# Where the split activations begin in SBUF: new start places for H, L, HH, HL and for the small matmul operands, in a float32r transformer kernel

## The reference

```
# first block (depth 1)
h = rms_norm(x);  proj = h @ w_in + b_in            # 1024 -> 4864
x += (gated sum of an RWKV-7 branch and an RG-LRU branch) @ w_mix_out
x += cross_attention(rms_norm(x), rms_norm(mem))    # w_cq, w_ckv, w_co
x += (gelu(conv(h @ w_in[:2816])) * h @ w_in[2816:]) @ w_ffn_out
# second block (depth 2), for each layer
x += 0.5 * norm(swiglu(norm(x), w13, w2))           # stage a: 1024 -> 2 x 2816 -> 1024
x += norm(token_mixing(norm(x)))                    # stage m: three attentions, gates, w_out
x += norm(cross_attention_2(norm(x), norm(mem)))    # stage c
x += 0.5 * norm(swiglu(norm(x), w13, w2))           # stage b
```

## Time and profile before

| | |
|---|---|
| time, median of 3 runs (lowest to highest) | 2054.82 us (2053.24 to 2056.61) |
| the profiled execution | 2060.7 us |
| its span, first to last instruction | 2058.5 us |
| PE busy | 2021.5 us (98%) |
| DVE busy | 1353.8 us (66%) |
| ACT busy | 1090.1 us (53%) |
| share of PE in the chain that ended last | 90% |
| granted TensorE clock over the span | 0.999 |

### The profile page before, as it was taken

One profiled execution on the slowest core, in us unless ns is written; L12 is line 12 of the kernel. 1 busy time (PEld: TensorE's weight loads), 2 busy tenths in 40 slices (PEclk: granted clock), 3 DMA queues, 4 the chain that ended last, 5 costly groups with the idle time before them and its releaser, 6 DMA issues.

```text
span 2058.5 us, 34241 instructions
## 1 busy us (share of the span) xinstructions
PE 2021.5 (98%) x13588; PEld 1798.6 (87%) x13588; DVE 1353.8 (66%) x1909; ACT 1090.1 (53%) x1739; POOL 50.0 (2%) x47
## 2 busy tenths in 40 slices
PE   7999999999999999999999999999999999999998
PEld 7989988999888889899988888888899999887887
DVE  6776866777566667866766554655477677756554
ACT  5846555554454454555456444644454555645443
POOL 0021000000000000000100000000000001000000
PEclk9999999999999999999999999999999999999999
DMA  7522444555465546533553655555555534445553
GB/s 271 170 75 80 159 171 167 191 198 190 169 215 188 187 163 228 183 130 128 194 196 134 218 180 189 180 203 183 186 194 191 174 122 166 160 161 191 185 184 123
DMA packets 98716, 359.08 MB, mean 174 GB/s; under 512 B 11192, under 2 KB 11512, under 8 KB 98296
## 3 DMA queue, kind: packets, MB, share of 16 engines
q1 hardware_dynamic: 98560, 356.90, 50.5%
HBM read 353.65 MB, written 1.05 MB: 172 GB/s over the span
## 4 chain that ended last, share of the span: by engine, by line
PE 90%; DVE 5%; ACT 4%; issue 1%; DMA 0%; DVEq 0%; SPq 0%; ACTq 0%
PE ps L988 10%; PE ps L990 9%; PE ps L989 9%; PE ps L976 8%; PE ps L1166 8%; PE ps L1168 8%; PE ps L1167 8%; PE ps L1053 6%; PE ps L1055 6%; PE ps L1054 6%; DVE wlo L1658 2%; PE ps L1020 2%; PE ps L1021 2%; PE ps L1022 2%; PE ps L1135 1%; PE ps L1136 1%
## 5 line engine op out<-in xcount | busy, mean ns | idle before, releaser
L1658 DVE TENSOR_TENSOR wlo<-raw,whi 128x1024 fp32r<-128x1024 f32 x635 | 773.9, 1227 | 414.4 <-ACT whi L2390 411.7
L2390 ACT ACTIVATE whi<-raw 128x1024 fp32r<-128x1024 f32 x635 | 666.4, 1057 | 416.0 <-PE ps L1055 152.3
L988 PE MATMUL ps<-H,whi 128*128 128x256 f32 x1328 | 382.4, 288 | 2.3 <-DVE wlo L1658 2.2
L990 PE MATMUL ps<-H,wlo 128*128 128x256 f32 x1328 | 374.1, 282 | 0.0
L989 PE MATMUL ps<-L,whi 128*128 128x256 f32 x1328 | 374.0, 282 | 0.0
L1166 PE MATMUL ps<-whi,H 128*128 128x512 f32 x704 | 280.4, 398 | 4.9 <-DVE wlo L1658 2.4
L1168 PE MATMUL ps<-whi,L 128*128 128x512 f32 x704 | 276.4, 393 | 0.0
L1167 PE MATMUL ps<-wlo,H 128*128 128x512 f32 x704 | 276.0, 392 | 0.0
L988 PEld LDWEIGHTS ps<-H,whi 128*128 128x128 f32 x1328 | 251.6, 189 | 8.1 <-issue 4.4
L989 PEld LDWEIGHTS ps<-L,whi 128*128 128x128 f32 x1328 | 253.0, 191 | 0.5
L990 PEld LDWEIGHTS ps<-H,wlo 128*128 128x128 f32 x1328 | 251.7, 190 | 0.0
(11 more groups left out here) (438 smaller groups left out, 3275.6 us busy)
## 6 DMA issues: line engine op xcount, KB each, us to landing
raw<-in_ws SPq DMA_DIRECT2D x635, 512.0 KB, 3.3
prow<-in_rows SPq DMA_DIRECT2D x11, 512.0 KB, 5.6
row<-in_rows SPq DMA_DIRECT2D x9, 512.0 KB, 6.1
mema<-in_memT SPq DMA_DIRECT2D x4, 512.0 KB, 4.8
mema<-in_mem2T SPq DMA_DIRECT2D x4, 512.0 KB, 6.4
memb<-in_mem2T SPq DMA_DIRECT2D x4, 512.0 KB, 5.3
DT<-in_dec SPq DMA_DIRECT2D x2, 768.0 KB, 6.3
X<-in_x SPq DMA_DIRECT2D x1, 1024.0 KB, 10.7
```

What stands on the lines that cost most here:

```text
L988: e.matmul(o, h, hs[k], start=first and k == 0, stop=False, skip_group_check=True)
L990: mm = e.matmul(o, lo, hs[k], start=False, stop=last and end, skip_group_check=True)
L1658: e.tensor_tensor(m.wlo[:, n % SPL, :], r, h.bitcast(F32), SUB).then_inc(*c.lo.done(n))
L2390: e.activation(m.whi[:, n % SPL, :], m.raw[:, n % RAW, :], ACT.Copy).then_inc(*c.hi.done(n))
```

## The change

The lanes go. A table `BEGIN` gives each stage a place in bytes for `H` and another for `L`; a table `HIDDEN` does so for `HH` and `HL`. Most of the places are not multiples of 64, or are unlike for high and low. The mixers' output product gets places of its own (key `("o", l)`), where it shared `mix`. Eight of the small operands' pairs begin 64 bytes later (`SIDE`), and the stores of `HH` and `HL` get 256 bytes of slack, by which everything behind them moves on (`SPREAD`).

```
-LANE, LANES = 16, 8
-LANE_OF = {"x0": 1, "mix": 0, "c": 2, "f": 3, ("a", 0): 0, ("m", 0): 4, ("c", 0): 5, ("b", 0): 1, ("a", 1): 2, ("m", 1): 6,
-           ("c", 1): 7, ("b", 1): 4}
+SLACK, SIDE = 256, 64
+SPREAD = (16, 40, 58, 82.5)
+BEGIN = {"x0": (64, 192), "mix": (16, 16), "c": (64, 0), "f": (32, 32), ("a", 0): (32, 32), ("m", 0): (96, 96), ("o", 0): (0, 32), ("c", 0): (64, 128), ("b", 0): (224, 224), ("a", 1): (0, 64), ("m", 1): (160, 160), ("o", 1): (32, 0), ("c", 1): (224, 224), ("b", 1): (96, 96)}
+HIDDEN = {"f": (160, 160), ("a", 0): (192, 192), ("b", 0): (0, 128), ("a", 1): (64, 0), ("b", 1): (0, 192)}
...
-        self.H_store = kept("H", [128, 8 * T + LANES * LANE], F32R)
-        self.L_store = kept("L", [128, 8 * T + LANES * LANE], F32R)
+        self.H_store = kept("H", [128, 8 * T + SLACK // 4], F32R)
+        self.L_store = kept("L", [128, 8 * T + SLACK // 4], F32R)
...
-        def at(name, kb, shape, dt=F32):
-            off = low + (int(kb * 1024) + 63) // 64 * 64
+        def at(name, kb, shape, dt=F32, lane=0):
+            kb += sum(SLACK for start in SPREAD if kb >= start) / 1024
+            off = low + (int(kb * 1024) + 63) // 64 * 64 + lane
...
-                     for x, kb, kb2 in (("a", 16, 24), ("b", 98.6, 58.5))]
+                     for x, kb, kb2, lane in (("a", 16, 24, SIDE), ("b", 98.6, 58.5, 0))]
...
-        self.HH, self.HL = at("HH", 42.5, [128, 22, T], F32R), at("HL", 64.5, [128, 22, T], F32R)
+        self.HH_store, self.HL_store = (at(n, kb, [128, 22 * T + SLACK // 4], F32R) for n, kb in (("HH", 42.5), ("HL", 64.5)))
...
-        self.YH, self.YL = two("YH", 62, 2, half, F32R), two("YL", 58, 2, half, F32R)
+        self.YH, self.YL = two("YH", 62, 2, half, F32R, SIDE - SLACK), two("YL", 58, 2, half, F32R, SIDE - SLACK)
...
-        self.BH, self.BL = at("BH", 110.2, four, F32R), at("BL", 114.2, four, F32R)
+        self.BH, self.BL = at("BH", 110.25, four, F32R, SIDE), at("BL", 114.25, four, F32R, SIDE)
...
-        self.QH, self.QL = at("QH", 8, [128, 3, T], F32R), at("QL", 11, [128, 3, T], F32R)
+        self.QH, self.QL = at("QH", 8, [128, 3, T], F32R, SIDE), at("QL", 11, [128, 3, T], F32R, SIDE)
...
-        self.BRH = [at(f"BRH{n}", kb, four, F32R) for n, kb in enumerate((50.5, 8, 74.5))]
-        self.BRL = [at(f"BRL{n}", kb + 4, four, F32R) for n, kb in enumerate((50.5, 8, 74.5))]
+        self.BRH = [at(f"BRH{n}", kb, four, F32R, SIDE) for n, kb in enumerate((50.5, 8, 74.5))]
+        self.BRL = [at(f"BRL{n}", kb + 4, four, F32R, SIDE) for n, kb in enumerate((50.5, 8, 74.5))]
...
-        return self.lane(self.H_store, LANE_OF[s])
+        return self.begun(self.H_store, 8, BEGIN[s][0])
...
-        return self.lane(self.L_store, LANE_OF[s])
+        return self.begun(self.L_store, 8, BEGIN[s][1])
+    def hidden_high(self, s):
+        return self.begun(self.HH_store, 22, HIDDEN[s][0])
+    def hidden_low(self, s):
+        return self.begun(self.HL_store, 22, HIDDEN[s][1])
+    def begun(self, store, n, at):
+        return store[:, at // 4:at // 4 + n * T].rearrange("p (k t) -> p k t", k=n)
```

More of the change, by code:

```diff
@@ L814, in at, with two @@
             return nc.alloc_sbuf_tensor_at(name, shape, dt, offset=off)
-        def two(name, kb, step, shape, dt=F32):
-            return [at(f"{name}{i}", kb + step * i, shape, dt) for i in range(2)]
+        def two(name, kb, step, shape, dt=F32, lane=0):
+            return [at(f"{name}{i}", kb + step * i, shape, dt, lane) for i in range(2)]
         full8, half, four = [128, 8, T], [128, 2, T], [128, 4, T]
         self.K, self.VV = at("K", 0, full8), at("VV", 8, [128, 2, 1024])
-        self.mems = [[at("mem" + x, kb, full8), at("mh" + x, kb2, full8, F32R), at("ml" + x, kb2 + 8, full8, F32R)]
-                     for x, kb, kb2 in (("a", 16, 24), ("b", 98.6, 58.5))]
+        self.mems = [[at("mem" + x, kb, full8), at("mh" + x, kb2, full8, F32R, lane), at("ml" + x, kb2 + 8, full8, F32R, lane)]
+                     for x, kb, kb2, lane in (("a", 16, 24, SIDE), ("b", 98.6, 58.5, 0))]
         self.smm, self.rbm = at("smm", 40, [128, T]), at("rbm", 41, [128, T])
@@ L846, in __init__ @@
         self.msk = at("msk", 53, [128, NMSK - 1024])
-        self.GG, self.BO, self.YA = two("GG", 58, 2, half), two("BO", 62, 2, half), two("YA", 66, 2, half)
-        self.YH, self.YL = two("YH", 62, 2, half, F32R), two("YL", 58, 2, half, F32R)
+        self.GG, self.BO, self.YA = two("GG", 58, 2, half, lane=SIDE - SLACK), two("BO", 62, 2, half, lane=SIDE - SLACK), two("YA", 66, 2, half)
+        self.YH, self.YL = two("YH", 62, 2, half, F32R, SIDE - SLACK), two("YL", 58, 2, half, F32R, SIDE - SLACK)
         self.PX, self.PY = at("PX", 70, [128, 4, T + 3]), at("PY", 74.1, four)
@@ L868, in __init__ @@
         self.swapped = {"rq": at("RS", 16, four), "qa": at("QS", 20, [128, 1, T]), "mq": at("MS", 24, full8), "dq": at("DS", 32, full8)}
-        self.QH, self.QL = at("QH", 8, [128, 3, T], F32R), at("QL", 11, [128, 3, T], F32R)
-        self.rbq, self.rbk = at("rbq", 14, [128, T]), at("rbk", 15, [128, T])
+        self.QH, self.QL = at("QH", 8, [128, 3, T], F32R, SIDE), at("QL", 11, [128, 3, T], F32R, SIDE)
+        self.rbq, self.rbk = at("rbq", 14, [128, T], lane=SIDE), at("rbk", 15, [128, T], lane=SIDE)
         self.GT = [[at(f"GT{n}{i}", 16 + 8 * n + 2 * i, half) for i in range(4)] for n in range(3)]
@@ L885, in high @@
     def high(self, s):
-        return self.lane(self.H_store, LANE_OF[s])
+        return self.begun(self.H_store, 8, BEGIN[s][0])
     def low(self, s):
-        return self.lane(self.L_store, LANE_OF[s])
-    def lane(self, store, n):
-        return store[:, LANE * n:LANE * n + 8 * T].rearrange("p (k t) -> p k t", k=8)
+        return self.begun(self.L_store, 8, BEGIN[s][1])
[5 more added lines that the diff above has]
+        return store[:, at // 4:at // 4 + n * T].rearrange("p (k t) -> p k t", k=n)
     def mem(self, i):
@@ L1035, in outward @@
         if kind == "m":
-            return 8, "w_out_2", s[1], m.high("mix"), m.low("mix"), lambda k: dve.after("ml2", s[1], k // 2)
+            return 8, "w_out_2", s[1], m.high(("o", s[1])), m.low(("o", s[1])), lambda k: dve.after("ml2", s[1], k // 2)
         if kind == "c":
@@ L1040, in outward @@
         name, layer = ("w_ffn_out", 0) if s == "f" else ({"a": "ffn1_w2_2", "b": "ffn2_w2_2"}[kind], s[1])
-        return 22, name, layer, m.HH, m.HL, lambda k: dve.after("hl", s, k // 2)
+        return 22, name, layer, m.hidden_high(s), m.hidden_low(s), lambda k: dve.after("hl", s, k // 2)
     def columns_of(s, name, layer, k, col):
@@ L2092, in fin_rest @@
         e.wait_ge(*act.after("hh", s, j))
-        tt(m.HL[:, 2 * j:2 * j + 2, :], m.UP[j % 2][:, :, :], m.HH[:, 2 * j:2 * j + 2, :].bitcast(F32), SUB, ("hl", s, j))
+        tt(m.hidden_low(s)[:, 2 * j:2 * j + 2, :], m.UP[j % 2][:, :, :], m.hidden_high(s)[:, 2 * j:2 * j + 2, :].bitcast(F32), SUB, ("hl", s, j))
     def fin_out(s, p):
@@ L2127, in hidden_turned @@
         e.wait_ge(*act.after("hh", s, g))
-        tt(m.HL[:, 2 * g:2 * g + 2, :], pair(banks.of("ht", s, g)), m.HH[:, 2 * g:2 * g + 2, :].bitcast(F32), SUB, ("hl", s, g))
+        tt(m.hidden_low(s)[:, 2 * g:2 * g + 2, :], pair(banks.of("ht", s, g)), m.hidden_high(s)[:, 2 * g:2 * g + 2, :].bitcast(F32), SUB, ("hl", s, g))
         banks.free(dve, "ht", s, g)
@@ L2355, in merged @@
         e.wait_ge(*act.after("mh2", l, i // 2))
-        stt(m.low("mix")[:, i:i + 2, :], m.MG[:, i:i + 2, :], 0.5, m.high("mix")[:, i:i + 2, :].bitcast(F32), MUL, SUB, ("ml2", l, i // 2))
+        stt(m.low(("o", l))[:, i:i + 2, :], m.MG[:, i:i + 2, :], 0.5, m.high(("o", l))[:, i:i + 2, :].bitcast(F32), MUL, SUB, ("ml2", l, i // 2))
     run = {"first": first, "mem": mem, "jy": jy, "jx": jx, "jn": jn, "jh": jh, "mem_rms": mem_rms, "keys_out": keys_out, "mem_cols": mem_cols,
@@ L2719, in fin_out @@
             e.wait_ge(*dve.after("up", s, j))
-            do(m.HH[:, 2 * j:2 * j + 2, :], m.UP[i][:, :, :], ACT.Copy, ("hh", s, j))
+            do(m.hidden_high(s)[:, 2 * j:2 * j + 2, :], m.UP[i][:, :, :], ACT.Copy, ("hh", s, j))
     def wide_out(s, g):
@@ L2730, in hidden_turned @@
         e.wait_ge(*pe.after("ht", s, g))
-        do(m.HH[:, 2 * g:2 * g + 2, :], pair(banks.of("ht", s, g)), ACT.Copy, ("hh", s, g))
+        do(m.hidden_high(s)[:, 2 * g:2 * g + 2, :], pair(banks.of("ht", s, g)), ACT.Copy, ("hh", s, g))
     def angles(p):
@@ L2862, in merged @@
         e.wait_ge(*dve.after("mg", l, 2, i))
-        do(m.high("mix")[:, i:i + 2, :], m.MG[:, i:i + 2, :], ACT.Copy, ("mh2", l, i // 2), scale=0.5)
+        do(m.high(("o", l))[:, i:i + 2, :], m.MG[:, i:i + 2, :], ACT.Copy, ("mh2", l, i // 2), scale=0.5)
     run = {"first": first, "mem": mem, "mem_rms": lambda i: root(("mem_rms", i), 1024),
```

## The result

The changed kernel takes 2068.29 us (median of 4 runs, 2067.22 to 2069.28), the kernel before beside it 2055.04 (2053.24 to 2056.61, 4 runs). The ratio is 1.0065, 95% interval 1.0047 to 1.0082: slower by 13.2 us. That is inside the stated range, and slower where "no change, leaning slower" was the likeliest.

A forecast was written before the change was run, and what follows sets the result against it. PE was taken as the bound, through the distances between matmul starts. Moving terms of -3.0 and stationary terms of +6.6 gave +3.6 us, on the median of 2054.8 a forecast of 2058.4 us; range 2044 to 2076.

The forecast's parts named there:

- no change, leaning slower: Whole kernel: likeliest reading of the +3.6 us sum; chances 0.36 no change, 0.39 slower, 0.25 faster.
- The small operands: Moving operands going from place 0 to 64: 1512 matmuls at -2.0 ns each, -3.0 us.
- the fast pace: Rival for moving stages: 113 ns taken more often; 2033 us if all, 2046 if half; chance 0.26.
- the stationary ones: Stages with the activation stationary: leaving place 0 costs time, +6.6 us in sum.
- the place alone: All matmuls: the operand's start place modulo 256 sets the distance; 64 costs 5.8 ns over 0 when stationary.
- f was to lose 1.3 us: Stage f, moving, from place 192 to 32: +1.2 ns for each of 1056 matmuls, +1.3 us.
- the midway value: Places without a row take the mean of known neighbours, such as stationary 32 at +2.9 ns, 224 at +2.3.
- two thirds: Unlike high and low places: high part weighs two thirds, low a third; hidden (64, 0) +1.0 us.
- One distance for each moving place: Moving stages: one value per place, 0: 120.0, 64: 118.0, 128: 118.9, 192: 117.8 ns.
- The 113 of x0: Stage x0 at place 64: a later stretch at 112.8 ns, against 118.2 earlier in the same stage.
- The extra step for places between multiples of 64: Rival, both forms: unaligned places pay 7 ns per matmul; 2097 us, one form 2074 to 2082; chance 0.18.
- The place is not the cause: Rival: stages differ by what else runs, so no effect, 2054.8 us; chance 0.06.

The follow-up runs named there:

- old_places: Changed kernel with the places of the kernel before put back (modulo 256), moved stores kept; 2059.12 us, ratio 1.0000 to the kernel before.
- stationary_zero: Changed kernel with the stationary operands of the wide stages, mix, output products and hidden layers back at place 0; 2050.50 us, ratio 0.9961 to the kernel before.
- weights_64: Changed kernel's code with whi and wlo beginning 64 bytes later, SIDE 0 and other places in its tables; 2059.34 us, 1.0020 of the kernel before.
- survey: Changed kernel with places not seen so far, such as moving 16 and 32, stationary 4, 8, 48 and 240; 2055.83 us, kernel before 2059.43.
- alike: Changed kernel with each low part put at its high part's place; 2061.76 us against 2067.37 for the changed kernel in the same set.
- small_only: As old_places, but with the small operands 64 bytes further; 2051.47 us, ratio 0.9966 to the kernel before.

## Why the prediction came out as it did

**What held.** The mechanism: PE's distances are the whole of what the profiles show, no other engine changed, and DVE and ACT wrote `L` and `H` in 684 and 591 ns (686 and 591 before). The place counts modulo 256 (old_places). The small operands gained by leaving 0 as moving operands (-3.7 us, -3.0 said, a part of it as keys came to the fast pace), the stationary ones lost; both together made the kernel slower, and with the stationary operands at 0 it was faster than before (stationary_zero). But the place alone, as I had put it, is not what counts: it is the place relative to the other operand's (weights_64), which no stage of the kernel before or after could tell from the place itself.

The Trainium skill (TensorE: Matmul & The Clock Gate, Step-by-step: what each phase is for) says that loading the next stationary operand takes no read bandwidth from the running matmul. The traces speak against it for these matmuls: in weights_64 hidden ("a", 0) stayed where it was, only the weights began 64 bytes later, and the distance went from 226.7 to 228.8 ns.

**What was luck.** The forecast of 2058.4 us was 9.9 too low; the measured time lies in the range of 2044 to 2076 since that was drawn wide, for rivals that didn't happen. Of the 9.9, 4.3 are the distances (+7.9 for +3.6). Most of the rest is that I let the changed kernel's profiled execution stand 5.9 us above its median because the kernel before's did; it stood at its median (2068.19, 2068.29). And the errors of the moving side helped to hide those of the stationary one: f was to lose 1.3 us and gained 1.2.

**The terms that were mis-sized.** (1) "For a place between two known ones I take the midway value." That is the step that failed most, for moving operands too (96 goes at 120.0 ns, not 118.45; 32 at 116.6, not 119.2). For stationary ones 32 costs 5.5 ns in ("a", 0), not 2.9; 224 costs 5.2, not 2.3 (both from the 92.0 and 91.9 us above); 160 costs 6.6, not 4.5. 192, set at 4.5, costs 2.1 in the hidden layer and 1.3 in a wide stage. (2) "For an unlike pair I weigh the high part by two thirds": (0, 128) costs 231.1 - 226.7 = 4.4 ns, not 1.5, (64, 0) 6.6, not 3.9, and (128, 0) in the survey 6.6, not 3.0. alike gained 4.3 us in the stages concerned where thirds would gain 1.3. (3) One distance for each moving place: f took 113.4 or 117.8 at 192 and 113.4 or 116.6 at 16, so a term of 1056 matmuls carries a spread of 3.5 to 4.7 us that place alone doesn't settle. The 113 of x0 was in the rows, and I priced it only as a rival.

**The rivals.** The extra step for places between multiples of 64 is no rule (240 is free, 8 costs 2.6, and moving operands pay none), but on the stationary side it was nearer for most of them than midway. For f the fast pace came only in small_only and the survey; in the changed kernel only keys from `mha`, just ahead of f, ran at it (durations of 276 ns). "The place is not the cause" fell with old_places against stationary_zero.

**What stays open.** Why the kernel before takes 2053.6 to 2055 us in some sets and 2059 in others, when the changed kernel took 2067 to 2068 both times, each beside the kernel before at 2054 to 2055; it was not run where that takes 2059, so what the change costs there is not known. The granted clock doesn't settle it: at a mean of 0.999 the kernel before took 2052.8 to 2054.3 us in the second set and 2057.2 to 2060.9 in the third. The clock does spread the runs within a set (old_places 2057.7 to 2059.8 at 0.999, 2061.0 and 2062.0 at 0.997). Open too is what sets the pace of a moving stage, and why most stationary places cost what they do: 16 cost 0, 3.7 and 6.6 ns in three stages.

## What to carry to other kernels

When PE is the bound and its clock is full, compare the start-to-start distance of the same line between stages: what differs there with the same shapes may be in the addresses. In this kernel it paid to put the stationary operand and the moving stream at the same place modulo 256 bytes when 512 columns move, with both parts of a high and low pair at it, and apart when 256 move. Don't interpolate between places: none of the midway values for stationary ones held. Judge such a change on several executions, more than one set of them, and by stage sums, since a long stage can have another pace in another set, by more than the change gives.

## What the runs showed of the hardware

- The distance between float32r matmuls depends on (moving start - stationary start) modulo 256 bytes, as far as weights_64 turned it: with 512 columns 226.7 ns at 0, and with the stationary operand at 240 in the survey, mostly 228.8 to 234 elsewhere; with 256 columns 120.0 at 0, 113.4 to 118.9 at most others, but 120.0 at 96 too. In the survey a stationary operand 4 bytes off cost 7.5 ns, one 8 bytes off 2.6.
- The steadiest values, 113.3, 120.0, 226.7 and 233.3 ns, are 17, 18, 34 and 35 times 6.67 ns. Others are means over a pattern: f at 117.8 goes 117, 118, 118, 119, ("m", 0) at 96 repeats 125, 115, 124, 118, 121, 117 (mean 120.0).
- The same moving place has two paces, and the same kernel at the same place took 107.8 and 112.0 us for a stage in two sets, on two chips.
- The kernel before took 2059.4, 2053.6 and 2059.1 us in three sets on three chips, each within 5 us of itself: more between sets than the 0.2% that I had taken for the limit of the measurement. Whether it is the chip that does it, no run shows.
